# Reordering the products that run beside the second scan of a mixer layer

## The chip, the cores and the metric

The kernel runs on one core of one Trainium2 chip. The metric is the device time of one execution in microseconds (us). Three runs of the kernel before gave 2110.74, 2112.5 and 2116.45 us; the median is 2112.5 us.

## What is computed

The reference is a two-layer mixer block followed by an attention and mixture-of-experts block, for one sequence of 256 tokens and a width of 1024. The change touches only the two layers of the first block. There, one normalised input `u` is multiplied with the columns of one wide weight, and the pieces go to three branches whose results are gated and added:

```python
h = rmsnorm(x)                      # u in the kernel
z, xbc, dt, q, f, i, g, mq, mk, mv, ig, fg, mo, gates = split(h @ w_in)
y_ssd = ssd_branch(z, xbc, dt)      # two-way state space scan, then a gated norm
y_hg  = hgrn2_branch(q, f, i, g)    # two-way gated linear scan
y_ml  = mlstm_branch(mq, mk, mv, ig, fg, mo)
merged = (sigmoid(gate_s) * (y_ssd @ w_br_ssd)
          + sigmoid(gate_h) * (y_hg @ w_br_hg)
          + sigmoid(gate_m) * (y_ml @ w_br_ml))
x = x + merged @ w_out
```

The arithmetic is in fp32. The products written as `@` above are of 256 tokens with 1024 by 1024 slices of weights.

## The kernel before, in words

**Units.** All weights come from one stream in HBM, cut into units of 1 MB (128 partitions by 2048 numbers). A unit makes 256 output columns: it lands in one of four slots of `ring`, TensorE multiplies it with `u` or with a branch's result, the sum stands in one of three PSUM banks `G`, and ScalarE or VectorE reads it out and frees the bank. `KINDS` (line 49) is the list of units in order: `mq`, `mk`, `mv`, `mo` are the four inputs of the third branch, `gs` is the gate of the state space branch, `bs` its output weight, `gh` and `gm` are the other gates, `bh` and `bm` the other output weights. `OF`, `POS`, `USE` and the packing of the stream on the host follow from that list.

**Plain and split units.** A plain unit is 32 fp32 matmuls (line 1040, or 969 for the units that are laid out by token). A split unit is 48 faster matmuls in three groups of 16: high part of the weights by high part of `u`, high by low (both line 1030, or 1018 and 1023 for the first unit of a kind), and low part of the weights by high part of `u` (line 1035). For those, ScalarE copies the weights into a rounded high part (`hi`, line 2006, signal `whi_ok`) and VectorE subtracts it to get the low part (`lo`, line 2683, signal `wlo_ok`). TensorE waits for `whi_ok` ahead of the unit and for `wlo_ok` ahead of its last third. Line 2010 makes the high part of `u` (`u_high`) and line 2391 the low part (`u_low`). `mo`, `gs` and the first two `gh` are split (list `SCAN`, line 105); `mq`, `mk`, `mv` and `bs` are plain. `WSCAN` (line 326) says where in the arena each of these ten units has its high part.

**The second scan.** The hgrn2 branch is worked out in 18 levels k, nine for each half of the heads. Level k has arguments (`hgA`, VectorE lines 2541 to 2546), exponentials (ScalarE lines 1956 to 1958), operands (`hgB`, VectorE lines 2561 to 2564), small products (`hgB`, TensorE lines 1228, 1239, 1248) and a copy of the result (`hgC`, VectorE lines 2577 to 2600). After level 17 come the last output products (`ho`, TensorE line 1260, ScalarE line 1962), the squares (ScalarE line 1965), their sums (`hnorm`, TensorE line 1266), and on ScalarE four logarithms and four exponentials (lines 1969 and 1973), then on VectorE eight scalings and one multiplication (lines 2606 and 2610).

**The order by hand.** The order of all work of a layer is one list, `sched` (from line 632). Each engine walks through the same list and does its own part of every item. The part that matters is a loop over i from 2 to 23, one step for each of the units `mq + i`. In step i TensorE multiplies unit `mq + i`; VectorE does `hgA` of level i-1, `hgB` of level i-2 and `hgC` of level i-3; TensorE then does the small products of level i-2. At the end of a step the unit's bank is read (`read`). `hi` and `lo` of a unit stand one step ahead of it.

In the kernel before, steps 12 to 15 are the four `mo` units and steps 16 to 23 are `gs` and `bs` in turn:

```python
+ ["mq"] * 4 + ["mk"] * 4 + ["mv"] * 4 + ["mo"] * 4
+ ["gs", "bs"] * 4 + ["gh"] * 4 ...
```

So splits of weights stand in steps 11 to 15, 17, 19, 21 and 23. The sigmoid of all of `mo` (`msig`) stands in step 16. A `gs` unit is read by ScalarE, which writes its sigmoid to `MERGED`; a `bs` unit is then read by VectorE (line 2274), which multiplies it onto `MERGED`.

Of the kernel before, what the change touches and what calls it, by code (L numbers as in the profile page):

```python
# [20 lines left out]
ACT = mybir.ActivationFunctionType  # L21
AX_X = mybir.AxisListType.X

P = 128
D = 1024
# [24 lines left out]
         + ["mq"] * 4 + ["mk"] * 4 + ["mv"] * 4 + ["mo"] * 4  # L50
         + ["gs", "bs"] * 4 + ["gh"] * 4 + ["gm"] * 4 + ["bh"] * 4 + ["bm"] * 4
# [199 lines left out]
def program(nc, stream, par_d, con_d, x_d, par2_d, con2_d, out, upto=None):  # L251
    ctx = ExitStack()
    with ctx:
# [72 lines left out]
        WSCAN = (HF, 122, HF, 122, HF, HF, HF, HF, 42, 0)  # L326
# [106 lines left out]
        def signal(name, per_layer, credit=0):  # L433
            return Signal(sem(name), per_layer, credit)
# [50 lines left out]
        yln = signal("ssd_logs_ready", 1)  # L485
# [33 lines left out]
        merge_ok = signal("merged_ready", 4)  # L519
        silu_ok = signal("ffn_silu_ready", 22)  # L520
# [13 lines left out]
        lam_in, lam_mm, lam_exp = sem("lambda_products"), sem("lambda_sums"), sem("lambda_exponentials")  # L534
# [128 lines left out]
        gh, gs, mo = OF["gh"], OF["gs"], OF["mo"]  # L663
        for i in range(2, 24):
            if i in (17, 19, 21):
                sched.append(("hi", gs + i - 15))
            elif i == 23:
                sched.append(("hi", gh))
            elif 11 <= i <= 15:
                sched.append(("hi", mo + i - 11 if i < 15 else gs))  # L670
            if i == 12:
                sched.append(("u_low", 0))
# [35 lines left out]
            if k - 2 == 17:  # L708
                sched.append(("ho", 1))
# [1062 lines left out]
        def _(act):  # L1772
            st = Steps(act, act_step)

            def unit(lay, n):
                kind, j = KINDS[n], n - OF[KINDS[n]]
                j = j // 2 if kind in ("gs", "bs") else j
                if kind in ("rows", "bs", "bh", "bm", "out", "down") or kind in ("hi", "mv") and j % 2 == 0:
                    return
# [32 lines left out]
                else:  # L1812
                    dst = {"z": Z, "hf": HF, "hq": HQ, "hg": HG, "mq": MQ, "mk": MK, "mo": MO,
                           "gs": MERGED, "gh": GH, "gm": GM, "pleg": PLG}[kind]
                    func = {"z": ACT.Silu, "gs": ACT.Sigmoid, "gh": ACT.Sigmoid, "gm": ACT.Sigmoid,
# [32 lines left out]
            def item(kind, k, lay):  # L1848
# [114 lines left out]
                elif kind == "hnorm":  # L1963
                    act.wait_ge(ho_cp.sem, ho_cp.at(lay, 4))
                    act.activation(flat(HE[0], KC), flat(HQ, KC), ACT.Square).then_inc(hsq.sem, 1)
                    prime()
# [26 lines left out]
                elif kind in ("split", "hi"):  # L1993
# [101 lines left out]
            act.activation(small[:, 2:4], A[3][:, 0:2], ACT.Exp).then_inc(lam_exp, 1)  # L2095
# [127 lines left out]
        def _(dve):  # L2223
# [23 lines left out]
            def unit(lay, n):  # L2247
                kind, j = KINDS[n], n - OF[KINDS[n]]
                j = j // 2 if kind in ("gs", "bs") else j
                if kind not in ("rows", "bs", "bh", "bm", "out", "down", "xbc", "up"):  # L2250
                    return
# [10 lines left out]
                dve.wait_ge(unit_done.sem, unit_done.at(lay, POS[n] + 1))  # L2262
# [9 lines left out]
                elif kind == "bs":  # L2272
                    dve.wait_ge(*evac(lay, n - 1))
# [467 lines left out]
            dve.wait_ge(lam_exp, 1)  # L2741
# [503 lines left out]
```

## Time and profile before

| what | value |
| --- | --- |
| median of three runs | 2112.5 us |
| time of the profiled execution | 2116.87 us |
| span of its profile | 2114.8 us |
| TensorE busy with matmuls | 1969.2 us (93%) |
| VectorE busy | 1271.7 us (60%) |
| ScalarE busy | 930.9 us (44%) |
| mean busy share of the 16 DMA engines in the slices of the two layers | 3 to 6 tenths |

The profiled execution took 2.1 us more than its span, and is 4.4 us above the median of the three runs. Times in the timeline are counted from the start of the span. The second scan of the first layer lies at about 220 to 412 us, that of the second layer at about 977 to 1169 us.

In the timeline a row is: start, duration of the group, engine, line, operation, what it writes and reads, the number of instructions, and in brackets how long the engine had been idle before it and what released it. A group's duration runs to the modelled end of its last matmul, so it can overlap the start of the next row by 0.1 to 0.4 us; the distance between two starts is the safer measure. A row of stretches has, for each engine, busy us with the number of instructions, then the granted TensorE clock as a share of full speed, the share of the DMA engines and the GB/s.

### The profile page before, as it was taken

What the parts mean: (1) busy time and instruction counts of PE and PEld (TensorE: products, weight loads), DVE (VectorE), ACT (ScalarE), POOL (GpSimd) and SP (SyncE); (2) the same over time, 40 slices, a digit from 0 to 9 for tenths busy, and PEclk for the clock granted to TensorE, in tenths of its full rate; (3) what the DMA queues carried; (4) which work ended last, traced back from release to release, by engine and by line L of the source; (5) the groups of instructions that cost most, each with busy time, mean ns of one, the idle gap of its engine ahead of it and who ended that gap; (6) DMA issues with size and microseconds to landing.
All of it is one profiled execution on the core that took longest, in us unless ns stands there. A gap on an engine that the chain in (4) does not pass through costs nothing. (4 is left out here: it accounts for less than half of the span.)

```text
span 2114.8 us, 48552 instructions
## 1 busy us (share of the span) xinstructions
PE 1969.2 (93%) x20908; PEld 1702.5 (81%) x20908; DVE 1271.7 (60%) x2183; ACT 930.9 (44%) x1162; POOL 31.3 (1%) x62
## 2 busy tenths in 40 slices
PE   8999999999999999999999999999999897777766
PEld 7998869999999999988689999999987664444433
DVE  6887879488677567896795796786543211111111
ACT  5544655574556355546464754664412210111101
POOL 0000000000000000000000000000000000000000
PEclk9999999999999999999999999999999898888897
DMA  6555344444555554553434544455787899999997
GB/s 236 181 204 192 124 160 154 169 176 179 180 180 188 199 182 174 211 193 140 176 127 158 199 163 177 179 183 197 269 333 287 335 373 422 422 422 422 422 422 326
DMA packets 71935, 498.91 MB, mean 236 GB/s; under 512 B 8448, under 2 KB 8576, under 8 KB 13536
## 3 DMA queue, kind: packets, MB, share of 16 engines
q1 hardware_dynamic: 66528, 479.57, 59.5%
q0 software_dynamic: 4384, 14.49, 2.0%
q8 instruction: 128, 2.10, 0.4%
q10 hardware_dynamic: 864, 2.49, 0.3%
q14 instruction: 31, 0.25, 0.0%
HBM read 495.38 MB, written 1.15 MB: 235 GB/s over the span
## 5 line engine op out<-in xcount | busy, mean ns | idle before, releaser
L2683 DVE TENSOR_TENSOR ring_r<-ring,weights_and_u_split 128x2048 fp32r<-128x2048 f32 x88 | 201.4, 2291 | 76.4 <-ACT weights_and_u_split L2006 72.7
L1035 PE MATMUL bank<-weights_and_u_split,ring_r 128*128 128x256 f32 x1880 | 246.3, 283 | 0.0
L1035 PEld LDWEIGHTS bank<-weights_and_u_split,ring_r 128*128 128x128 f32 x1880 | 234.8, 192 | 0.0
L1030 PE MATMUL bank<-weights_and_u_split,hidden_and_weights_high 128*128 128x256 f32 x1664 | 211.5, 284 | 0.0
L1030 PEld LDWEIGHTS bank<-weights_and_u_split,hidden_and_weights_high 128*128 128x128 f32 x1664 | 203.6, 192 | 4.8 <-issue 4.3
L2006 ACT ACTIVATE weights_and_u_split<-ring 128x2048 fp32r<-128x2048 f32 x88 | 167.6, 1907 | 53.5 <-PE bank L1035 46.6
L3044 DVE COPY arena<-bank 128x128 f32<-128x128 f32 x32 | 9.3, 292 | 293.4 <-PE bank L1651 293.4
L2183 ACT ACTIVATE arena<-bank 64x256 f32<-64x256 f32 x32 | 12.1, 377 | 350.8 <-PE bank L1633 350.8
L1633 PE MATMUL bank<-arena 128*32 128x256 f32 x1312 | 109.1, 466 | 59.4 <-DMA arena<-stream 55.4
L2683 DVE TENSOR_TENSOR ring_r<-ring,hidden_and_weights_high 128x2048 fp32r<-128x2048 f32 x64 | 146.2, 2286 | 29.3 <-ACT hidden_and_weights_high L2006 29.2
L2239 DVE SCALAR_TENSOR_TENSOR arena<-bank,par,arena 128x255 f32<-128x255 f32 (+1 forms) x272 | 111.3, 476 | 48.7 <-ACT arena L1809 48.5
L1633 PEld LDWEIGHTS bank<-arena 128*32 128x32 f32 x1312 | 49.6, 126 | 111.6 <-issue 76.4
L2006 ACT ACTIVATE hidden_and_weights_high<-ring 128x2048 fp32r<-128x2048 f32 x64 | 121.9, 1907 | 11.9 <-PE bank L957 8.5
L1822 ACT ACTIVATE arena<-bank 128x512 f32<-128x512 f32 x96 | 56.9, 593 | 153.4 <-PE bank L1035 140.7
L1030 PE MATMUL bank<-weights_and_u_split 128*128 128x256 f32 x840 | 117.8, 283 | 0.0
L1809 ACT ACTIVATE arena<-bank,par 128x256 f32<-128x256 f32 x112 | 57.1, 559 | 130.4 <-PE bank L1035 127.6
L1040 PE MATMUL bank<-u,ring 128*128 128x256 f32 x512 | 114.0, 381 | 0.0
L1030 PEld LDWEIGHTS bank<-weights_and_u_split 128*128 128x128 f32 x840 | 108.3, 192 | 0.0
L1040 PEld LDWEIGHTS bank<-u,ring 128*128 128x128 f32 x512 | 96.3, 190 | 13.8 <-issue 0.8
L1030 PE MATMUL bank<-u_r,weights_and_u_split 128*128 128x256 f32 x736 | 103.3, 283 | 0.0
L1030 PEld LDWEIGHTS bank<-u_r,weights_and_u_split 128*128 128x128 f32 x736 | 94.9, 192 | 0.0
L1633 PE MATMUL bank<-ring,arena 128*32 128x256 f32 x672 | 53.7, 447 | 39.0 <-DMA ring<-stream 39.0
(492 smaller groups left out, 3636.5 us busy)
## 6 DMA issues: line engine op xcount, KB each, us to landing
ring<-stream SPq DMA_DIRECT2D x320, 1024.0 KB, 4.9
arena<-stream SPq DMA_DIRECT2D x129, 1024.0 KB, 25.9
arena<-rows_scratch POOLq DMA_DIRECT2D x48, 256.0 KB, 4.7
place_of_rows<-stream SPq DMA_DIRECT2D x2, 1024.0 KB, 6.1
place_of_parameters<-stream SPq DMA_DIRECT2D x2, 1024.0 KB, 8.0
h<-x_d ACTq DMA_DIRECT2D x4, 256.0 KB, 4.7
ring<-stream ACTq DMA_DIRECT2D x1, 1024.0 KB, 9.3
u<-stream SPq DMA_DIRECT2D x1, 1024.0 KB, 6.9
```

Of the source, the lines that this page charges most:

```text
L1030: pe.matmul(bank[:, c * S:(c + 1) * S], whi[k][:, c * P:(c + 1) * P], yhi[k] if xx is None else xx[:, k, :], start=(sub == 0 and c == part ...
L1035: mm = pe.matmul(bank[:, c * S:(c + 1) * S], wlo[k][:, c * P:(c + 1) * P], yhi[k] if xhi is None else xhi[:, k, :], start=False, stop=(end ...
L1040: mm = pe.matmul(bank[:, c * S:(c + 1) * S], w[:, k, c * P:(c + 1) * P], x[:, k, :], start=(k == 0), stop=(k == KC - 1))
L1633: mm = pe.matmul(G[0][g:g + 32, 0:S], xe[:, 2 * j + k, a * SLOTS:(a + 1) * SLOTS], w[k][:, g * 8:g * 8 + S], start=(j == k == 0), stop=(j ...
L1809: a = act.activation(arena[:, dst, :], bank[:, c * S:(c + 1) * S], ACT.Identity, scale=pc(wn, ch * width + width // 2), bias=pc(bn, ch))
L1822: act.activation(flat(at, 2), bank[:, :], func).then_inc(f.sem, 1)
L2006: act.activation(high(k), scan_high_or_low(k, ring[:, POS[k] % RING, :]), ACT.Copy).then_inc(whi_ok.sem, 1)
L2183: act.activation(arena[0:64, SGE, :], G[0][0:64, 0:S], ACT.Silu).then_inc(sg_ok, 1)
L2239: ins = stt(o, bank[:, c * S + lo + d:c * S + hi + d], pc(wn, chans[c] * width + j), o, ALU.mult, ALU.add)
L2683: tt(scan_high_or_low(k, ring_r[:, POS[k] % RING, :]), scan_high_or_low(k, w), high(k).bitcast(F32), ALU.subtract)\
L3044: V.tensor_copy(flat(HTE, 1)[:, 0:4 * SLOTS], A[4][:, 0:4 * SLOTS]).then_inc(ht_cp, 1)
```

## The change

The order of the units becomes `mq`, `mk`, `mv`, then four `bs`, four `mo`, four `gs`, `gh`. The splits of weights stand in steps 15 to 23, one in each. The high part of `u` is made in step 13 and not 10, its low part at the head of step 14 and not 12, and `msig` stands in step 20. `bs` is read by ScalarE with a plain copy to `MERGED`. ScalarE writes the sigmoid of a `gs` unit back into its PSUM bank, and VectorE multiplies the bank with `MERGED` and frees it. The squares of the hgrn2 output are an item of their own, `hsquare`, at the end of step 20, while `hnorm` stays at the end of step 21. The places of the high parts change with the order. A semaphore for the lambda exponentials of the second block is merged into another one.

```diff
-         + ["mq"] * 4 + ["mk"] * 4 + ["mv"] * 4 + ["mo"] * 4
-         + ["gs", "bs"] * 4 + ["gh"] * 4 + ["gm"] * 4 + ["bh"] * 4 + ["bm"] * 4
+         + ["mq"] * 4 + ["mk"] * 4 + ["mv"] * 4 + ["bs"] * 4 + ["mo"] * 4
+         + ["gs"] * 4 + ["gh"] * 4 + ["gm"] * 4 + ["bh"] * 4 + ["bm"] * 4
...
-        WSCAN = (HF, 122, HF, 122, HF, HF, HF, HF, 42, 0)
+        WSCAN = (HF, Z) * 4 + (42, 0)
...
         for i in range(2, 24):
-            if i in (17, 19, 21):
-                sched.append(("hi", gs + i - 15))
-            elif i == 23:
-                sched.append(("hi", gh))
-            elif 11 <= i <= 15:
-                sched.append(("hi", mo + i - 11 if i < 15 else gs))
-            if i == 12:
+            if i >= 15:
+                sched.append(("hi", mq + i + 1))
+            if i == 14:
                 sched.append(("u_low", 0))
...
-            if i == 16:
+            if i == 20:
                 sched.append(("msig", 0))
-            if i in (17, 19, 21):
-                sched.append(("lo", gs + i - 15))
-            elif i == 23:
-                sched.append(("lo", gh))
-            elif 11 <= i <= 15:
-                sched.append(("lo", mo + i - 11 if i < 15 else gs))
-            if i == 10:
+            if i >= 15:
+                sched.append(("lo", mq + i + 1))
+            if i == 13:
                 sched.append(("u_high", 0))
...
             if k - 2 == 17:
-                sched.append(("ho", 1))
+                sched += [("ho", 1), ("hsquare", 0)]
...
# ScalarE, unit
+                    if kind == "gs":
+                        act.activation(bank[:, :], bank[:, :], ACT.Sigmoid).then_inc(gs_sig.sem, 1)
+                        return
                     dst = {"z": Z, "hf": HF, "hq": HQ, "hg": HG, "mq": MQ, "mk": MK, "mo": MO,
-                           "gs": MERGED, "gh": GH, "gm": GM, "pleg": PLG}[kind]
+                           "bs": MERGED, "gh": GH, "gm": GM, "pleg": PLG}[kind]
...
# ScalarE, item
-                elif kind == "hnorm":
+                elif kind == "hsquare":
                     act.wait_ge(ho_cp.sem, ho_cp.at(lay, 4))
                     act.activation(flat(HE[0], KC), flat(HQ, KC), ACT.Square).then_inc(hsq.sem, 1)
+                elif kind == "hnorm":
                     prime()
...
-                    if k == OF["gh"]:
-                        act.wait_ge(unit_done.sem, unit_done.at(lay, POS[OF["gs"] + 6] + 1))
-                    elif k == OF["gh"] + 1:
-                        act.wait_ge(unit_done.sem, unit_done.at(lay, POS[OF["bs"] + 6] + 1))
+                    if k == OF["mo"] + 1:
+                        act.wait_ge(unit_done.sem, unit_done.at(lay, POS[last("bs")] + 1))
...
# VectorE, unit
+                if kind == "gs":
+                    dve.wait_ge(gs_sig.sem, gs_sig.at(lay, j + 1))
+                else:
+                    dve.wait_ge(unit_done.sem, unit_done.at(lay, POS[n] + 1))
...
-                elif kind == "bs":
-                    dve.wait_ge(*evac(lay, n - 1))
+                elif kind == "gs":
+                    dve.wait_ge(*evac(lay, OF["bs"] + j))
                     tt(flat(MERGED + 2 * j, 2), bank[:, :], flat(MERGED + 2 * j, 2), ALU.mult).then_inc(f.sem, 1)
```

## Rows read from the trace of the kernel before

**Rows 1.** Stretches of the second scan, first layer: busy us of each engine
```profile
340.00:350.00 10.00, 9.30 (x114) 8.39 (x114) 9.43 (x16) 8.86 (x9) 0.00 (x0) 1.00 0.29 107
...
370.00:380.00 10.00, 10.00 (x63) 9.27 (x63) 0.03 (x1) 3.65 (x5) 1.95 (x4) 1.00 0.43 152
```
**Rows 2.** Waits of TensorE, 285 to 450 us: total us, times, longest
```profile
PE banks_by_token L1228 <- DVE arena L2564: 1.3, 2, 0.7
```
**Rows 3.** Timeline of TensorE, first layer, steps 13 to 18
```profile
316.09 1.22 PE L1030 MATMUL bank<-weights_and_u_split,hidden_and_weights_high 128*128 128x256 f32 x8
...
322.04 0.76 PE L1228 MATMUL banks_by_token<-arena 128*32 128x32 f32 x64
...
336.03 0.76 PE L1228 MATMUL banks_by_token<-arena 128*32 128x32 f32 x64 [0.64 <-DVE arena L2564]
...
343.44 0.76 PE L1228 MATMUL banks_by_token<-arena 128*32 128x32 f32 x64 [0.69 <-DVE arena L2564]
344.13 7.17 PE L1040 MATMUL bank<-arena,ring 128*128 128x256 f32 x32
351.23 1.15 PE L1239 MATMUL banks_by_token<-arena 128*64 128x64 f32 x32
352.31 1.22 PE L1030 MATMUL bank<-weights_and_u_split,scan_weights_high 128*128 128x256 f32 x8
```
**Rows 4.** Timeline of TensorE, second layer: the wait of step 15
```profile
1092.90 0.76 PE L1228 MATMUL banks_by_token<-arena 128*32 128x32 f32 x64 [0.64 <-DVE arena L2564]
```
**Rows 5.** Timeline of VectorE, first layer, steps 12 to 17
```profile
305.42 2.50 DVE L2391 TENSOR_TENSOR u_r<-u,weights_and_u_split 128x512 fp32r<-128x512 f32 x4 [0.94 <-PE bank L969]
...
323.61 0.69 DVE L2541 TENSOR_TENSOR arena<-arena 128x512 f32<-128x512 f32 x1
...
331.02 0.69 DVE L2541 TENSOR_TENSOR arena<-arena 128x512 f32<-128x512 f32 x1
...
344.24 0.69 DVE L2541 TENSOR_TENSOR arena<-arena 128x512 f32<-128x512 f32 x1 [0.50 <-PE banks_by_token L1228]
...
348.51 0.68 DVE L2564 TENSOR_TENSOR arena<-arena 128x512 f32<-128x512 f32 x1
...
350.26 2.29 DVE L2683 TENSOR_TENSOR ring_r<-ring,scan_weights_high 128x2048 fp32r<-128x2048 f32 x1
352.46 0.68 DVE L2274 TENSOR_TENSOR arena<-bank,arena 128x512 f32<-128x512 f32 x1
```
**Rows 6.** Timeline of TensorE, first layer, two plain units of the early steps
```profile
255.48 7.17 PE L1040 MATMUL bank<-u,ring 128*128 128x256 f32 x32
...
263.28 7.17 PE L1040 MATMUL bank<-u,ring 128*128 128x256 f32 x32
```
**Rows 7.** Timeline of TensorE, first layer, steps 22, 23 and the unit behind
```profile
387.52 1.30 PE L1030 MATMUL bank<-weights_and_u_split,scan_weights_high 128*128 128x256 f32 x8
...
393.46 7.07 PE L1040 MATMUL bank<-arena,ring 128*128 128x256 f32 x32
400.18 1.30 PE L1030 MATMUL bank<-weights_and_u_split,scan_weights_high 128*128 128x256 f32 x8
```
**Rows 8.** Timeline of ScalarE, first layer, steps 21 to 23
```profile
387.91 2.42 ACT L1969 ACTIVATE arena<-banks_by_token,eps 128x512 f32<-128x512 f32 x4 [4.87 <-PE banks_by_token L1266]
390.36 2.19 ACT L1973 ACTIVATE arena<-arena 128x512 f32<-128x512 f32 x4
392.57 1.28 ACT L1822 ACT_TABLE_LOAD   x1
393.87 0.60 ACT L1822 ACTIVATE arena<-bank 128x512 f32<-128x512 f32 x1
394.36 1.91 ACT L2006 ACTIVATE scan_weights_high<-ring 128x2048 fp32r<-128x2048 f32 x1
```
**Rows 9.** Timeline of VectorE, first layer, the low part behind the normalisation
```profile
396.53 2.29 DVE L2683 TENSOR_TENSOR ring_r<-ring,scan_weights_high 128x2048 fp32r<-128x2048 f32 x1
```
**Rows 10.** Stretches with idle TensorE: in the third branch, and in the second block
```profile
490.00:496.00 6.00, 4.60 (x52) 3.71 (x56) 5.35 (x8) 2.31 (x3) 0.00 (x0) 1.00 0.36 109
...
1660.00:1670.00 10.00, 6.97 (x189) 5.05 (x180) 2.40 (x13) 4.32 (x12) 0.00 (x0) 0.81 0.36 130
```

More of the change, by code:

```diff
@@ L484, in program @@
         yrs = signal("ssd_rstd_ready", 1)
-        yln = signal("ssd_logs_ready", 1)
+        yln = signal("ssd_logs_then_lambda_exponentials_ready", 1)
         ys_fin = signal("ssd_branch_ready", 1)
@@ L519, in program @@
         merge_ok = signal("merged_ready", 4)
+        gs_sig = signal("state_gate_sigmoids_ready", 4)
         silu_ok = signal("ffn_silu_ready", 22)
@@ L533, in program @@
         ada_cp, ada_mm = sem("modulation_rows_copied"), sem("modulation_columns_ready")
-        lam_in, lam_mm, lam_exp = sem("lambda_products"), sem("lambda_sums"), sem("lambda_exponentials")
+        lam_in, lam_mm = sem("lambda_products"), sem("lambda_sums")
         rope_mm, rope_ok = sem("rope_turned"), sem("rope_done")
@@ L662, in program @@
                   ("hclamp", 0), ("ssd_add", 0), ("hlog", 0), ("ssd_log", 0), ("hsilu", 0), ("read", mq + 1), ("hgK", 0)]
-        gh, gs, mo = OF["gh"], OF["gs"], OF["mo"]
+        gh = OF["gh"]
         for i in range(2, 24):
-            if i in (17, 19, 21):
-                sched.append(("hi", gs + i - 15))
-            elif i == 23:
-                sched.append(("hi", gh))
-            elif 11 <= i <= 15:
-                sched.append(("hi", mo + i - 11 if i < 15 else gs))
-            if i == 12:
+            if i >= 15:
+                sched.append(("hi", mq + i + 1))
+            if i == 14:
                 sched.append(("u_low", 0))
@@ L1776, in unit @@
                 kind, j = KINDS[n], n - OF[KINDS[n]]
-                j = j // 2 if kind in ("gs", "bs") else j
-                if kind in ("rows", "bs", "bh", "bm", "out", "down") or kind in ("hi", "mv") and j % 2 == 0:
+                if kind in ("rows", "bh", "bm", "out", "down") or kind in ("hi", "mv") and j % 2 == 0:
                     return
@@ L2094, in _ @@
             act.wait_ge(lam_mm, 1)
-            act.activation(small[:, 2:4], A[3][:, 0:2], ACT.Exp).then_inc(lam_exp, 1)
+            act.activation(small[:, 2:4], A[3][:, 0:2], ACT.Exp).then_inc(yln.sem, 1)
             if upto == "ada":
@@ L2248, in unit @@
                 kind, j = KINDS[n], n - OF[KINDS[n]]
-                j = j // 2 if kind in ("gs", "bs") else j
-                if kind not in ("rows", "bs", "bh", "bm", "out", "down", "xbc", "up"):
+                if kind not in ("rows", "gs", "bh", "bm", "out", "down", "xbc", "up"):
                     return
@@ L2261, in unit @@
                     return
-                dve.wait_ge(unit_done.sem, unit_done.at(lay, POS[n] + 1))
+                if kind == "gs":
+                    dve.wait_ge(gs_sig.sem, gs_sig.at(lay, j + 1))
+                else:
+                    dve.wait_ge(unit_done.sem, unit_done.at(lay, POS[n] + 1))
                 bank, f = G[USE[n] % GBANKS], freed[USE[n] % GBANKS]
@@ L2740, in _ @@
             first_norm()
-            dve.wait_ge(lam_exp, 1)
+            dve.wait_ge(yln.sem, yln.at(DEPTH, 1))
             st.done(tt(small[:, 4:5], small[:, 3:4], small[:, 2:3], ALU.subtract))
@@ L3143, in layer_units @@
     parts = [packed] + [(units_by_token if k in ("hi", "mv") else units)(seg[k])
-                             for k in ("z", "xbc", "hf", "hq", "hi", "hg", "mq", "mk", "mv", "mo")]
-    parts.append(np.stack([units(g[:, :D]), units(i["w_br_ssd"][lay])], 1).reshape(8, P, UNIT))
-    parts += [units(w) for w in (g[:, D:2 * D], g[:, 2 * D:], i["w_br_hg"][lay], i["w_br_ml"][lay], i["w_out"][lay])]
+                             for k in ("z", "xbc", "hf", "hq", "hi", "hg", "mq", "mk", "mv")]
+    parts += [units(i["w_br_ssd"][lay]), units(seg["mo"])]
+    parts += [units(w) for w in (g[:, :D], g[:, D:2 * D], g[:, 2 * D:], i["w_br_hg"][lay], i["w_br_ml"][lay], i["w_out"][lay])]
     parts.append(units(i["w_up"][lay].reshape(D, 2, FC, P).transpose(0, 2, 1, 3).reshape(D, FC * UC)))
```

2 lines of the change are left out of this document (1 added, 1 removed).

## The prediction

> **What bounds the kernel now.** I read the chip's own busy shares first, then the stretches of the second scan, then the waits of TensorE in it, then the timeline of each engine step by step. The stretches say that TensorE is full: 10.00 of 10 us in most of them and 9.30 in the worst, at the full clock. VectorE is nearly full beside it in the middle of the scan (9.43 of 10) and empty near its end (0.03 of 10) [rows 1]. The waits say what is to be had: in the whole stretch that the change reorders TensorE waits 1.3 us, in two waits, both for the scan's operands from VectorE [rows 2]. They stand in steps 15 and 16, 0.64 and 0.69 us [rows 3], and the second layer has the same two; its first is again 0.64 us [rows 4]. So a layer has 1.33 us to give and two layers 2.7 us, 0.13% of the time. About 0.3%, 6.3 us, is what a measurement of this kernel can tell from no change. The change adds no matmul and takes none away, so whatever it wins has to be one of these waits, and whatever it loses a new one.
>
> Why TensorE waits there: a VectorE step with a weight split takes 7.41 us (331.02 less 323.61) [rows 5], a TensorE step with a split unit 5.95 us (322.04 less 316.09) and 0.69 us for the small products (344.13 less 343.44) [rows 3], together 6.64. VectorE falls behind by 0.77 us a step, and five such steps in a row are more than its head start.
>
> **The change, part by part.** I count for one layer, and take the profiled execution's own time, 2116.87 us, as the base of the sum; the difference then goes onto the median 2112.5.
>
> *Plain `bs` units in steps 12 to 15.* A plain step with small products is 7.80 us on TensorE (263.28 less 255.48) [rows 6], against a VectorE step without a split of 7.41 less some 2.2 us, 5.2 us. `u_low`, 2.50 us [rows 5], now falls into step 14, which makes that one 7.7: just covered by 7.80. `u_high` on ScalarE moves from step 10 to 13, where ScalarE has only the three exponentials and a read. VectorE therefore enters step 15 level with TensorE. The two old waits go: **-1.33 us**.
>
> *The splits in steps 15 to 18.* Put the start of unit 15 at 0. VectorE's step 15 takes 7.41; TensorE's plain step ends at 7.80. Step 16: VectorE 7.9 to 15.3, TensorE to 14.44. Step 17: operands are ready 4.95 us into VectorE's step (348.51 plus 0.68 less 344.24) [rows 5], at 20.25, and TensorE's unit ends at 20.39: still no wait. But this step has the long copy at the end of the small levels, so it takes 8.22 us (352.46 less 344.24) [rows 5] and ends at 23.5. TensorE's unit 18 starts at 20.39 + 1.08 (352.31 less 351.23) [rows 3] = 21.47 and ends at 27.42; the operands of level 16 are there at 23.5 + 4.95 = 28.45. **A new wait of 1.0 us** in step 18, behind VectorE's backlog: the queue is the same as before, only later. Behind it VectorE has no more arguments to make and catches up. Its bounds: 0 if VectorE's head start is a microsecond more than I think, 1.5 if step 14 does not quite hold `u_low`.
>
> *The last `gs` unit behind the normalisation.* Before, unit 23 is plain and needs nothing from the other engines. Now it is split, and its high part stands on ScalarE behind the four logarithms and four exponentials of `hnorm`. Put the start of unit 22 at 0 (387.52). The exponentials end at 390.36 + 2.19, that is 5.03 [rows 8]; the copy takes 1.91 [rows 8], to 6.93; TensorE is through with unit 22 at 5.94 (393.46 less 387.52) [rows 7]. **A new wait of 1.0 us**, with all later matmuls queued behind it. Then VectorE: it has the whole normalisation ahead of the low part, whose subtraction ends at 396.53 + 2.29, that is 11.30 [rows 9]. TensorE, started at 6.93, is through two thirds of the unit (3.97 of 5.95) at 10.90. **A second wait of 0.4 us.** Bounds for the two together: 0.9 (the copy overlaps the exponentials' end, and the subtraction is just in time) and 1.9 (a table load or a read slips in between).
>
> *What ScalarE and VectorE swap.* `bs` is read by ScalarE in steps with little work: 0.60 us each [rows 8], hidden by the plain unit. `gs` is held by a sigmoid of 0.60 and then a multiplication of 0.68 [rows 5, 8] and has two units' time, over 11 us, before its bank is needed; in step 22 VectorE comes to it at 11.3, behind the low part, and the bank is wanted by the second `gh` unit at about 19. Cost nothing; if that cover were gone it would be what VectorE is late. The sigmoid of the last `gs` unit stands ahead of the split of `gh` + 1, where a plain unit had no work on ScalarE: 0.60 us in front of a chain (split, decays, split, high part of `u`) whose end TensorE meets just in time after two more units. In the new kernel TensorE is itself later there. I take **+0.1 us**, bounds 0 and 0.6.
>
> *Squares ahead.* Left in `hnorm`, they would stand behind the read of unit 21, which now waits on ScalarE for TensorE to finish that unit; TensorE would then meet the sums without their input. Moved, they are done during unit 21. Nothing won against before, where TensorE did not wait there either.
>
> *Seams.* A plain unit ahead of scan products takes 7.11 us (7.80 less 0.69), one ahead of a split unit 6.72 (400.18 less 393.46) [rows 6, 7]; the four now all stand in the first place. The split units get part of it back. **+0.1 us**, bounds -0.3 and +0.7.
>
> *The table loads.* One is 1.28 us [rows 8]. They become fewer in steps 16 to 19 and stand where ScalarE has time. *The lambda semaphore, the places of the high parts, the order of the stream:* each unit's slot is still freed four units ahead, the same bytes move, and each place is still reused two units later; the first use of `Z` waits for the last `bs`, which is over as the split begins. Nothing. The gpsimd queue is not passed by anything: its rows for the third branch wait for the last output products, as before.
>
> Sum for a layer: -1.33 + 1.0 + 1.0 + 0.4 + 0.1 + 0.1 = +1.27 us; for two, +2.5 us. The profiled execution would go from 2116.87 to 2119.4, the median from 2112.5 to **2115.0 us**. The parts' bounds leave each layer between -0.7 (-1.33 + 0 + 0.9 + 0 - 0.3) and +3.4 (-1.33 + 1.5 + 1.9 + 0.6 + 0.7), so 2111.1 to 2119.3.
>
> **The rivals.** *Forecast, 0.63:* two old waits traded for later ones, a small loss, 2115.0.
>
> *Covered, 0.25.* The backlog does not build up, because VectorE enters step 15 early enough, and the normalisation's end leaves the last unit's high part in time. Then only the removal counts: -2.7 us, 2109.8. For it: the new order plainly spreads the splits, and steps 12 and 13 have over 2 us of slack each on VectorE. Against it: slack does not carry over, since `hgA` waits for the small products of two levels before, and ScalarE's queue is in order, so the copy cannot pass the exponentials [rows 8].
>
> *The clock falls, 0.07.* The place is step 23 (and 18), where TensorE now stands idle for 1.0 us in each. If the granted clock fell there, the units behind would run slower. The price from a row: a stretch of 10 us at a mean of 0.81 is 1.9 us of full-speed work lost [rows 10]; one at each of the four new places makes 7.6 us, and with the 2.5 us of waits +10.1 us, 2122.6. It decides as soon as such stretches cost over 1 us each. Against it: in the six us from 490, TensorE is idle for 1.40 and the clock stays at 1.00; it is 0.81 only where TensorE was busy for 7 of 10 us [rows 10]. The Trainium skill has the rule that speaks for this rival ("TensorE: Matmul & The Clock Gate", section "HAM oscillation — how this bites in real kernels"): idle gaps between groups of matmuls can throw the array back to half rate, and every following group starts cold. By that rule the time would be this rival's 2122.6; the trace does not show it at gaps of this size.
>
> *None of these, 0.05:* scatter of a median (the three runs differ by 5.7 us), half to either side.
>
> Faster by over 0.3% would be below 2106.2. No wait in the rows is large enough for it; I give 0.04 for scatter. Slower by over 0.3%, above 2118.8: the clock, and the top of my bounds, 0.09. The rest, 0.87, is the same. The range takes in the covered case and my own bounds and half a microsecond to a microsecond of scatter on either side: 2109.0 to 2120.0; the forecast's own range is 2111.1 to 2119.3.
>
> **What would show it.** Right: no wait of TensorE on line 2564 in the first two `mo` steps, one of about 1.0 us ahead of line 1239 in the step of the third `mo` unit; a wait of about 1.0 us on line 2006 ahead of the fourth `gs` unit and one of about 0.4 us on line 2683 inside it; from the first unit of the second scan to the first `gh` unit 1.3 us more than before, in both layers alike. Wrong: no wait there (then the time falls to 2110), a wait at the sums of squares on line 1266, a wait for a bank of `gs`, a granted clock under 1.00 between 300 and 420 us, or a wait of TensorE in step 14 for operands held up by `u_low`.

## The result, and the profile after

The changed kernel takes **2117.05 us** (median of 21 runs, 2110.99 to 2121.79), the kernel before 2112.0 us (21 runs beside them, 2107.94 to 2118.51). The ratio of the two is 1.0019, with a 95% interval of 1.001 to 1.0027: 4.0 us slower, between 2.1 and 5.7. By the bound of 0.3% that is no change that counts, and with this many runs it is still a small loss that is surely there. The forecast was 2115.0 and "a small loss". One execution of the kernel of experiment 8 took 4119.39 us; it stands in no median and no ratio here.

The waits of TensorE are the view that the forecast was about. This is the kernel after, from 220 to 480 us; the columns are engine and line, what it waited for, total us, times, longest us.

```profile
PE banks_by_token L1232 <- DVE arena L2560: 1.1, 1, 1.1
PE banks_by_token L1221 <- DVE arena L2560: 1.0, 2, 0.7
PE bank L1023 <- ACT hidden_low L2000: 0.8, 1, 0.8
PE bank L1028 <- DVE ring_r L2679: 0.4, 1, 0.4
PE bank L1011 <- ACT hidden_low L1901: 0.3, 1, 0.3
```

The numbers of lines are smaller than before by 7 on TensorE (1239 is now 1232, 1228 is 1221, 1030 is 1023, 1035 is 1028, 1018 is 1011), by 6 for the high part (2006 is 2000) and by 4 on VectorE (2564 is 2560, 2683 is 2679). The group of L1221 stands ahead of 285 us, in steps that the change leaves alone; the kernel before has it too (in the second layer it lists 2.3 us in 4 waits on that line, of which 1.33 are the two of the middle). So the two waits of [rows 2] are gone and four new ones stand there: 1.1, 0.8, 0.4 and 0.3 us. The second layer has the same list, with 0.9 for L1221. None of the waits is in step 14 (`u_low`), at the sums of squares or for a bank of `gs`, the three places that the forecast named as signs of being wrong.

The timeline of TensorE in the first layer, kernel after, shows where they are. The columns are start, duration, engine, line, operation, out<-in, and in brackets the idle time ahead of it and what ended it.

```profile
356.95 2.08 PE L1028 MATMUL bank<-weights_and_u_split,ring_r 128*128 128x256 f32 x16
360.13 1.15 PE L1232 MATMUL banks_by_token<-arena 128*64 128x64 f32 x32 [1.10 <-DVE arena L2560]
...
387.08 1.30 PE L1023 MATMUL bank<-weights_and_u_split,scan_weights_high 128*128 128x256 f32 x8
...
391.10 2.08 PE L1028 MATMUL bank<-weights_and_u_split,ring_r 128*128 128x256 f32 x16
393.97 1.22 PE L1023 MATMUL bank<-weights_and_u_split,hidden_low 128*128 128x256 f32 x8 [0.79 <-ACT hidden_low L2000]
...
398.43 2.18 PE L1028 MATMUL bank<-weights_and_u_split,ring_r 128*128 128x256 f32 x16 [0.36 <-DVE ring_r L2679]
400.45 1.12 PE L1023 MATMUL bank<-weights_and_u_split,scan_weights_high 128*128 128x256 f32 x8
...
413.26 2.91 PE L1011 MATMUL bank<-hidden_low,scan_weights_high 128*128 128x256 f32 x16 [0.26 <-ACT hidden_low L1901]
```

The first is in step 18, ahead of the small products. Then the last `gs` unit: TensorE waits for its high part, starts it at 393.97, does two thirds, and waits again, until 398.43, for its low part. The fourth is ahead of the split of `u` for the third branch.

ScalarE and VectorE at the last `gs` unit, kernel after, same columns:

```profile
387.47 2.42 ACT L1965 ACTIVATE arena<-banks_by_token,eps 128x512 f32<-128x512 f32 x4 [1.57 <-PE banks_by_token L1259]
389.92 2.19 ACT L1969 ACTIVATE arena<-arena 128x512 f32<-128x512 f32 x4
392.02 1.90 ACT L2000 ACTIVATE hidden_low<-ring 128x2048 fp32r<-128x2048 f32 x1
...
396.09 2.28 DVE L2679 TENSOR_TENSOR ring_r<-ring,hidden_low 128x2048 fp32r<-128x2048 f32 x1
```

Logarithms, exponentials and the copy of the high part stand one behind the other without a gap (387.47 to 393.92), and TensorE starts 0.05 us behind the copy. The subtraction ends at 398.37, and TensorE goes on at 398.43. Both queues run in order, and the normalisation stands ahead in each.

The stretches of the kernel after at the two places; the columns are stretch, its length, busy us (instructions) of TensorE, weight loads, VectorE, ScalarE and GpSimd, the granted clock, DMA share and GB/s.

```profile
356.00:362.00 6.00, 4.90 (x64) 4.63 (x63) 5.96 (x9) 4.23 (x5) 0.00 (x0) 1.00 0.38 111
392.00:398.00 6.00, 5.21 (x42) 4.87 (x41) 5.96 (x7) 5.61 (x5) 0.00 (x0) 1.00 0.50 175
```

The clock stays at 1.00 in both, which is 2.4 GHz, and so does its mean over the whole of 20 to 1640 us.

**Where the time went.** Differences of starts in the timeline of TensorE, between marks that both kernels have, tell more than idle rows. The marks of the first layer are the first `ho` product (306.00 before, 304.72 after) and the first product of the third branch (411.88 and 411.97, line 1278 or 1271). I take the same pair in the second layer, and from the first mark on to the router's products, where the next part begins.

| us | layer 1 | layer 2 | first `ho` to router | router to end | span |
|---|---|---|---|---|---|
| before | 105.88 | 105.87 | 1338.04 | 470.76 | 2114.8 |
| after | 107.25 | 107.24 | 1341.52 | 464.96 | 2111.2 |

The change costs 1.37 us in each layer and 3.48 us up to the router. The part behind the router, which the change does not touch, was 5.8 us shorter in the profiled execution of after, so that its span is the shorter one although the kernel is slower. That part was between 463.0 and 470.8 us in the twelve traces of this study, whatever the kernel. Two traces of one kernel (experiments 2 and 3) differ by 0.17 us from the first `ho` product to the router and by 2.6 us behind it. So from here on I compare traces up to the router and whole kernels by their ratios. A single time says little: 21 runs of the kernel before are spread over 10.6 us.

### The profile page after: what moved, and what is told of

Its sections match the earlier page's. It is cut to its first block and busy times, and to the rows that moved or that the text cites. A ratio compares the mean times of both kernels' runs of the same rounds, so it can differ in the third digit from the quotient of the medians.

```text
span 2111.2 us, 48556 instructions
## 1 busy us (share of the span) xinstructions
PE 1963.3 (93%) x20908; PEld 1697.2 (80%) x20908; DVE 1271.7 (60%) x2183; ACT 930.9 (44%) x1166; POOL 31.4 (1%) x62
## 3 DMA queue, kind: packets, MB, share of 16 engines
HBM read 495.38 MB, written 1.15 MB: 235 GB/s over the span
## 5 line engine op out<-in xcount | busy, mean ns | idle before, releaser
L1023 PE MATMUL bank<-weights_and_u_split,hidden_and_weights_high 128*128 128x256 f32 x1600 | 202.1, 284 | 0.0
L1023 PEld LDWEIGHTS bank<-weights_and_u_split,hidden_and_weights_high 128*128 128x128 f32 x1600 | 195.4, 192 | 4.7 <-issue 4.3
L2679 DVE TENSOR_TENSOR ring_r<-ring,hidden_and_weights_high 128x2048 fp32r<-128x2048 f32 x60 | 137.0, 2286 | 29.1 <-ACT hidden_and_weights_high L2000 29.0
L2000 ACT ACTIVATE hidden_and_weights_high<-ring 128x2048 fp32r<-128x2048 f32 x60 | 114.4, 1908 | 12.9 <-PE bank L950 8.5
```

The costliest lines, as they stand in the source:

```text
L1023: pe.matmul(bank[:, c * S:(c + 1) * S], whi[k][:, c * P:(c + 1) * P], yhi[k] if xx is None else xx[:, k, :], start=(sub == 0 and c == part ...
L2000: act.activation(high(k), scan_high_or_low(k, ring[:, POS[k] % RING, :]), ACT.Copy).then_inc(whi_ok.sem, 1)
L2679: tt(scan_high_or_low(k, ring_r[:, POS[k] % RING, :]), scan_high_or_low(k, w), high(k).bitcast(F32), ALU.subtract)\
```

## Experiments

**The theory:** the order of work on ScalarE and VectorE makes the loss. The two parts (high and low) of unit 23's weights stand behind the normalisation (about 1.15 us of waiting a layer), VectorE's backlog stands in step 18 (1.1 us), and the old waits (1.33 us) went since there are plain units there. **The rivals:** the order of units itself (the seams between split and plain ones) costs time; a wait sets the clock down; or these waits cover each other, so that taking one away only moves it.

**1. Squares back in the normalisation.** What did the squares' new place buy?

```
             if k - 2 == 17:
-                sched += [("ho", 1), ("hsquare", 0)]
+                sched.append(("ho", 1))
             if k - 3 == 17:
-                sched.append(("hnorm", 0))
+                sched += [("hsquare", 0), ("hnorm", 0)]
```

> The new order with the squares put back to the head of hnorm, behind the read of unit 21. My theory: ScalarE's queue is in order, so the squares start only when TensorE is through with unit 21 and its sigmoid is read (0.58 us), and take 1.91 us; TensorE then waits about 2.5 us ahead of the sums of squares in each layer, the rest of the chain moves back with it, and the waits ahead of and inside the last gs unit stay at 0.8 and 0.4 us. From the head of the output products of the first half to the first gh unit a layer takes 2.5 us more than in the changed kernel. Rival (the squares were never at stake, as TensorE did not wait for them before the change either): no wait there, no difference.

Measured: 2125.13 us beside 2113.32 of the kernel before, one run each. ScalarE's and TensorE's rows at the sums, and the stretches around them, in this kernel; the last stretch is the one behind the same wait in layer 2:

```profile
384.62 1.90 ACT L1960 ACTIVATE arena<-arena 128x2048 f32<-128x2048 f32 x1
386.58 5.19 PE L1259 MATMUL banks_by_token<-arena,con 128*128 128x256 f32 x16 [2.48 <-ACT arena L1960]
```

```profile
384.00:387.00 3.00, 0.52 (x2) 0.42 (x2) 0.69 (x1) 2.85 (x3) 0.00 (x0) 0.86 0.57 171
387.00:390.00 3.00, 3.00 (x9) 2.38 (x9) 0.00 (x0) 0.83 (x1) 0.00 (x0) 0.57 0.44 186
390.00:393.00 3.00, 3.00 (x21) 2.79 (x20) 0.00 (x0) 1.20 (x3) 0.00 (x0) 1.00 0.00 0
...
1151.00:1154.00 3.00, 3.00 (x9) 2.37 (x8) 0.00 (x0) 0.00 (x0) 0.00 (x0) 0.50 0.10 41
```

The wait of 2.48 us is as forecast. But a layer is 4.2 us longer than in the kernel after (111.46 against 107.25), not 2.5. The rest is the granted clock: 0.57 (near the lower level of 1.2 GHz) in the three us from 387, where the wait has just ended (386.58), so that the 16 sums take 5.19 us, against 3.62 in the kernel after. That is 1.6 us more for the same matmuls. So the rival of the falling clock was a real one, only not at the waits that this change makes. And the squares' place is a needed part of the new order: without it the two layers lose 8.7 us more (1350.21 less 1341.52).

**2 and 3. The last split ahead of the normalisation.** The high and the low part of unit 23 are moved from behind `hnorm` to just ahead of it. Nothing else changes. The third run is the same kernel with more executions.

```
-            if i >= 15:
+            if i >= 15 and i != 22:
                 sched.append(("hi", mq + i + 1))
...
-            if i >= 15:
+            if i >= 15 and i != 22:
                 sched.append(("lo", mq + i + 1))
...
             if k - 3 == 17:
-                sched.append(("hnorm", 0))
+                sched += [("hi", mq + i + 2), ("lo", mq + i + 2), ("hnorm", 0)]
```

> The new order with the split of the last gs unit, high and low part, put ahead of the normalisation on ScalarE and VectorE. My theory: the waits of 0.79 and 0.36 us ahead of and inside that unit go, in both layers, since the copy (1.9 us) now runs while TensorE forms the sums of squares (3.3 us); the logarithms may start 0.3 us later, which nobody meets. A layer is 1.1 to 1.2 us shorter. Rival (the normalisation is the limit): the wait moves to the first gh unit or to the third branch, and the layer is no more than 0.3 us shorter.

> The changed kernel with only the last gs unit's split put ahead of the normalisation, timed. Its trace, with one wait of 1.07 us and one of 0.26 us left, had the stretch from the first output product of the second scan to the third branch of the second layer at 862.5 us, against 862.7 before and 865.9 in the changed kernel. Expected: within 0.1% of the kernel before, that is, the loss of the change is gone with this one placement. Rival (the loss is in the order or in the tail, not in these waits): 0.1% to 0.2% slower than before, as the changed kernel.

Measured: 2109.67 us beside 2113.32 in the first, one run each; in the second 2112.85 us (12 runs, 2108.99 to 2117.76) beside 2112.61 of before (29 runs): ratio 1.0001, 0.9991 to 1.0012. The waits of TensorE from 300 to 420 us in it:

```profile
PE banks_by_token L1232 <- DVE arena L2560: 1.1, 1, 1.1
PE bank L1011 <- ACT hidden_low L1901: 0.3, 1, 0.3
```

Both waits of unit 23 are gone, and nothing took their place. A layer falls from 107.25 to 105.55 us, by 1.70 where 1.1 to 1.2 was expected, and the stretch to the router from 1341.52 to 1338.14, which is that of before (1338.04). So moving one split gives back as much as the change lost: 3.4 us in the trace, 3.8 by the ratios (0.0018 of 2112, each of the two ratios uncertain by about 0.001). The waits of step 18 and behind the scan are still there; the two old waits that went pay for them.

**4. The low part of the third `mo` unit on GpSimd.** Does VectorE's backlog make the wait of step 18? If so, 2.3 us less for VectorE should end it. In the kernel after, VectorE leaves out the subtraction of that unit, and GpSimd's queue, which is free there, does it with the same two semaphores (VectorE also waits for it ahead of its next subtraction, which the cut below leaves out):

```
+                k = OF["mo"] + 2
+                pool.wait_ge(wlo_ok.sem, wlo_ok.at(lay, NTH_SPLIT[k]))
+                pool.wait_ge(whi_ok.sem, whi_ok.at(lay, NTH_SPLIT[k] + 1))
+                pool.tensor_tensor(scan_high_or_low(k, ring_r[...]), scan_high_or_low(k, ring[...]),
+                                   high(k).bitcast(F32), ALU.subtract).then_inc(wlo_ok.sem, 1)
```

> The new order with the low part of the third mo unit's weights (128x2048, one subtraction) made by the idle gpsimd engine and not by VectorE. My theory, a backlog of VectorE: without 2.2 us of its step, the wait of 1.1 us ahead of the small products of level 16 goes; a layer is 1.1 us shorter, as long as the gpsimd subtraction takes under 9 us. Rival 1 (the wait is for something else, the exponentials or the copy of two levels before): it stays. Rival 2 (the gpsimd engine is slow or disturbs VectorE in SBUF): VectorE's own instructions beside it get longer than 0.69 and 1.22 us, or TensorE waits for the low part inside that unit, by the gpsimd duration less 9 us.

Measured: 2128.08 us beside 2113.32, the opposite of what the theory forecast, with a wait of 4.16 us. Rows of GpSimd, VectorE and TensorE in it:

```profile
348.04 4.66 POOL L892 TENSOR_TENSOR ring_r<-ring,scan_weights_high 128x2048 fp32r<-128x2048 f32 x1 [176.59 <-ACT scan_weights_high L2005]
348.28 4.97 DVE L2546 TENSOR_TENSOR arena<-arena 128x512 f32<-128x512 f32 x1
353.18 0.68 DVE L2547 TENSOR_TENSOR arena<-arena 128x512 f32<-128x512 f32 x1
355.51 0.68 DVE L2565 TENSOR_TENSOR arena<-arena 128x512 f32<-128x512 f32 x1
356.25 1.98 PE L1237 MATMUL banks_by_token<-arena 128*64 128x64 f32 x32 [4.16 <-DVE arena L2565]
```

The same operands and the same products in the kernel after:

```profile
351.16 0.68 DVE L2560 TENSOR_TENSOR arena<-arena 128x512 f32<-128x512 f32 x1
351.93 1.15 PE L1232 MATMUL banks_by_token<-arena 128*64 128x64 f32 x32
```

A subtraction of 128x512 that takes VectorE 0.69 us takes 4.97 us while GpSimd subtracts: it ends 0.55 us behind GpSimd's end (348.28 and 4.97 is 353.25, GpSimd's is 352.70). This is the second rival of the expectation. VectorE was not made lighter: 2.3 us were taken off it and 4.3 us added, and the added part comes first. The wait is one step ahead of the one in question, in step 17. There TensorE had its operands just in time (351.84, and the products start at 351.93); now they come at 356.19. The last row of this kernel shows a second thing, 1.98 us for 32 small products that take 1.15 in the kernel after. The stretches of this kernel:

```profile
352.00:356.00 4.00, 0.09 (x1) 0.00 (x0) 4.00 (x5) 2.11 (x4) 0.70 (x1) 0.87 0.63 219
356.00:360.00 4.00, 3.75 (x40) 3.64 (x41) 3.01 (x7) 2.27 (x2) 0.00 (x0) 0.50 0.12 47
360.00:364.00 4.00, 4.00 (x29) 4.00 (x28) 4.00 (x7) 2.10 (x3) 0.00 (x0) 0.77 0.00 0
```

The clock is down again, behind a wait of 4.16 us. In step 18 TensorE then waits no more, but that does not answer the question: its unit starts 5.1 us later than in the kernel after (358.15, not 353.01) and VectorE's step only 3.2 (358.27, not 355.11). The run shows that a VectorE later by 4.35 us makes TensorE wait 4.16 us in step 17. What a lighter VectorE does to the wait of step 18 was not seen here.

**5. The same in the kernel before**, with the fourth `mo` unit, which stands ahead of the two old waits.

> The kernel before with the low part of the fourth mo unit's weights made by the gpsimd engine. Backlog theory: both old waits, 0.64 and 0.69 us in steps 15 and 16, go, in both layers, 1.33 us a layer, if the gpsimd subtraction takes under 8.5 us. Rival (gpsimd slow or disturbing): a wait of TensorE for the low part inside the fourth mo unit takes their place.

Measured: 2119.11 us beside 2113.32. The row of VectorE in it, and its wait:

```profile
324.17 4.97 DVE L2550 TENSOR_TENSOR arena<-arena 128x512 f32<-128x512 f32 x1
```

```profile
PE banks_by_token L1233 <- DVE arena L2569: 4.2, 1, 4.2
```

4.97 us again, to the hundredth. TensorE does not wait inside the `mo` unit, as the rival had it, but ahead of the small products of step 14. The two waits of [rows 3] are not in its list from 285 to 450 us: they stand behind this one, which put TensorE back more than VectorE, and there VectorE waits for TensorE (0.84 and 1.32 us). GpSimd is no helper for VectorE in either order.

**6. Operands of the second scan first (after).** Another way to bring the operands earlier: in each step `hgB` of the level that TensorE needs next goes ahead of `hgA` of the one behind it. No work is added.

```
             k = i - HG_DELAY
+            if 0 <= k - 1 < HSTEPS:
+                sched.append(("hgB", k - 1))
             if 0 <= k < HSTEPS:
...
-            if 0 <= k - 1 < HSTEPS:
-                sched.append(("hgB", k - 1))
             if i == 9:
```

> The new order, with VectorE making the operands of level k-1 ahead of the arguments of level k in every step of the second scan (two items of the list swapped, the same work). Backlog theory: the wait of 1.1 us ahead of the small products of level 16 is VectorE's lateness of about 1 us at the end of a queue that has 2.5 us of arguments in front of the operands; with the operands 2.5 us earlier in the step it goes, and so do the two waits of 0.68 and 0.27 us of the early steps: 2.0 us less in a layer, of which 1.1 between the output products and the third branch. Rival (the operands wait for the exponentials, which now end late): the waits stay or new ones appear in steps without a split, by up to 1.8 us each.

Measured: 2123.37 us (one run) beside 2111.69 (18 runs). All waits for scan operands are gone, the one of step 18 as well, and a layer falls from 107.25 to 106.08 us. That answers what the fourth run left open: with the same work in another order on VectorE the wait goes. Only the 0.8 and the 0.4 of unit 23 are left in the scan. But a new one of 4.2 us a layer stands in the early steps. The next run shows it.

**7. The same swap in the kernel before**, timed.

> The kernel before with the same swap of two items. Backlog theory: its four waits in a layer (0.68, 0.27, 0.64 and 0.69 us) go, 2.3 us a layer, 4.6 us in all, 0.22% faster; the stretch from the output products to the third branch is 1.3 us shorter in each layer. Rival: exponentials late, no gain.

Measured: 2119.82 us (12 runs, 2116.39 to 2127.47) beside 2111.69 (18 runs), ratio 1.004, 1.0026 to 1.0053: 0.4% slower where 0.22% faster was expected. The rows of ScalarE and TensorE around its only wait:

```profile
269.50 0.63 ACT L1956 ACTIVATE arena<-arena 128x512 f32<-128x512 f32 x1 [5.02 <-DVE arena L2546]
...
271.62 1.28 ACT L1947 ACT_TABLE_LOAD   x1
...
276.53 0.58 ACT L1822 ACTIVATE arena<-bank 128x512 f32<-128x512 f32 x1
277.16 6.36 PE L969 MATMUL bank<-ring,u 128*128 128x512 f32 x8 [4.19 <-ACT arena L1822]
```

and the stretches there:

```profile
275.00:278.00 3.00, 0.84 (x1) 0.50 (x2) 2.67 (x6) 2.98 (x3) 0.00 (x0) 0.62 0.00 0
278.00:281.00 3.00, 3.00 (x5) 1.28 (x4) 0.46 (x1) 2.50 (x4) 0.00 (x0) 0.50 0.00 0
281.00:284.00 3.00, 3.00 (x22) 1.21 (x23) 1.97 (x3) 0.00 (x0) 0.00 (x0) 0.74 0.00 0
```

In step 7 ScalarE has the step's three exponentials, then two long logarithms (`hlog` of the scan's second half, lines 1947 and 1948) with a table load, then the read of the unit's bank. That order is the same in both kernels. But with the swap VectorE makes the arguments behind the operands, so the exponentials start 8.03 us behind the start of the unit (269.50 less 261.47), where they start 3.13 us behind it in the kernel before (266.41 less 263.28), and the read comes later with them. TensorE wants that bank, waits 4.19 us, and the clock falls to 0.50: eight matmuls take 6.36 us, where they take 3.60 in the kernel before (274.61 to 278.21). The stretch of the scan itself is what the swap was made for: from the first `ho` product to the third branch it takes **104.40 us in both layers**, 1.48 less than before. The two waits that it took away have 1.33 us in their rows.

**8. Swap and early split together (after), timed.**

> The new order with the swap and with the last gs unit's split ahead of the normalisation. If the waits are all that can be mended, a layer is 1.1 + 0.95 + 0.79 + 0.36 us = 3.2 us shorter than in the changed kernel. Against the kernel before with the swap (all waits of both scans gone) it is then still behind by what the order itself costs TensorE, the seams and the 0.26 us behind the scan: 0.5 us a layer by the two traces, 0.1 us by my prediction. Rival (the new order frees something further on): it is level or ahead.

Measured: 2121.34 us (median of six runs, 2117.55 to 2123.81) beside 2111.69, ratio 1.0044, 1.0028 to 1.0059; the same wait of 4.2 us for the bank. Its layer takes 104.42 us, against 104.40 of the seventh run. With no wait left between these two marks the two orders of units are equal, to 0.02 us a layer. That is the answer on the seams: no cost can be seen. What the new order still has is the wait of 0.3 us behind the third branch's first product, outside these marks; up to the router it is 0.3 us longer in all (1341.59 against 1341.28).

**9 and 10. The swap without steps 7 to 10** (the logarithms stand in step 7), in the kernel before and in the kernel after with its early split. Both differ from runs 7 and 8 in one condition each:

```
-            if 0 <= k - 1 < HSTEPS:
+            if 0 <= k - 1 < HSTEPS and not 7 <= i <= 10:
                 sched.append(("hgB", k - 1))
...
-            if 0 <= k - 1 < HSTEPS:
+            if 0 <= k - 1 < HSTEPS and 7 <= i <= 10:
                 sched.append(("hgB", k - 1))
```

> The kernel before with operands ahead of arguments, but not in steps 7 to 10. The swap in step 7 put the exponentials, and behind them two logarithms, two table loads and the read of that step's bank later on ScalarE, and TensorE waited 4.2 us for the bank. Without it there I expect no wait of TensorE in either second scan: 2.3 us less in a layer than in the kernel before, 4.6 us in all, 0.2% faster. Rival: the waits of the steps that are swapped come back as bank waits elsewhere; then the time is the kernel's before or longer.

> The new order with operands ahead of arguments (not in steps 7 to 10) and the last gs unit's split ahead of the normalisation. Expected: no wait in the second scan, 3.2 us less in a layer than in the changed kernel, 6.4 us in all, so 2.9 us (0.14%) faster than the kernel before; but 0.4 to 0.6 us a layer behind the kernel before with its own swap, which is the price of the order itself. Rival: level with it.

Measured: the kernel before with the swap 2112.28 us (12 runs, 2108.39 to 2115.19), ratio 0.9996, 0.9986 to 1.0007: no difference that these runs can tell, where 4.6 us less was expected. The kernel after with swap and early split **2109.53 us** (12 runs, 2106.44 to 2113.94) beside 2112.61: ratio **0.9981, 0.9971 to 0.9992**. That is 4.0 us less, between 1.7 and 6.1, where 2.9 was expected. It is the fastest here and the only one whose interval lies below 1. The traces up to the router explain only 1.1 us of it (1338.04 less 1336.93); where the rest comes from, if it is more than scatter, is open. The waits of TensorE in it, from 220 to 480 us:

```profile
PE banks_by_token L1223 <- DVE arena L2562: 0.9, 1, 0.9
PE bank L964 <- ACT arena L1819: 0.9, 1, 0.9
PE bank L1013 <- ACT hidden_low L1903: 0.3, 1, 0.3
```

No wait was expected in either kernel. The first two are where the order of the two items changes back, at step 7; both kernels have them, and without them both might gain some 1.8 us a layer more. No run shows that. The table of the traces, in us ("both" is the swap and the early split together):

| kernel | layer 1 | layer 2 | first `ho` to router |
|---|---|---|---|
| squares back | 111.46 | 111.67 | 1350.21 |
| last split ahead | 105.55 | 105.58 | 1338.14 |
| last split ahead, second trace | 105.57 | 105.57 | 1338.31 |
| low part on GpSimd | 112.74 | 112.94 | 1352.86 |
| before, low part on GpSimd | 109.75 | 109.95 | 1346.30 |
| operands first | 106.08 | 106.07 | 1345.58 |
| before, operands first | 104.40 | 104.40 | 1341.28 |
| both | 104.42 | 104.42 | 1341.59 |
| before, operands first, not in steps 7 to 10 | 104.39 | 104.39 | 1336.07 |
| both, not in steps 7 to 10 | 104.42 | 104.41 | 1336.93 |

By this table the kernel before with the swap is 0.86 us shorter up to the router than the one that measured fastest, 0.43 us a layer, which is the price of the order that was expected (0.4 to 0.6). Nearly all of it lies behind the third branch's first product, where the wait of 0.26 us stands. By the medians the kernel before with the swap is 2.75 us slower. The intervals of the ratios overlap, so which of the two is faster stays open.

## Why the prediction was right, and where its terms were off

The forecast was the right case, and each of its waits stands where it was put, on the line and in the step that were named. The range of 2109.0 to 2120.0 took in the covered case too, so the time alone could not have told the two apart; the waits do. The whole was 1.5 us short by the ratio: +2.5 us forecast, +4.0 measured (2.1 to 5.7), 3.5 in the traces.

- *The old waits go, -1.33 us.* Right in place. By starts it is 1.48 a layer (105.88 less 104.40).
- *From the first unit of the second scan (unit 2) to the first `gh` unit, +1.3 us.* 1.56 in both layers (before 223.31 to 400.18, after 222.02 to 400.45). The next units, which now follow a split one, give 0.18 back up to the third branch.
- *Step 18, +1.0 us.* 1.10 in the row, and 1.18 by starts (353.01 to 360.13 is 7.12, the step before it 5.94). The working by VectorE's steps holds as well: its steps start at 339.47, 346.89 and 355.11 in the kernel after, 7.42 and 8.22 us apart, where the forecast took 7.41 and 8.22.
- *Unit 23, +1.0 and +0.4 us.* 0.79 and 0.36 in the rows, 0.95 and 0.72 by starts (387.08, 393.97 and 400.45, against 5.94 and 5.76 for such a unit without a wait). Both ends of the chain (copy behind the exponentials, subtraction behind the normalisation) are as forecast: 6.84 and 11.29 us behind the start of unit 22, where it had 6.93 and 11.30, and run 2 shows that their place is the cause.
- *Three waits together.* 2.4 us forecast, 2.25 in the rows, but **2.83 by starts** (107.25 less the 104.42 of the same units without them). This is where the sum was short, above all in the second wait of unit 23 (0.4 forecast, 0.72 measured) and in step 18. The old waits were priced at their idle rows, and a wait costs more than that: in the rows a group of matmuls reaches past the start of the next (398.43 and 2.18 is 400.61, but the next starts at 400.45), and the idle time ahead of a wait is counted from that late end. The group behind a wait is also 0.1 us longer between starts (398.43 to 400.45 is 2.02, where 404.29 to 406.21 is 1.92). Unit 23's two waits show both together: 1.15 us in the rows, 1.70 us won by removing them. Less the old waits' 1.48, the difference is 1.35 us a layer instead of 1.07.
- *Behind the scan, +0.1 us (0 to 0.6).* The place was the right one: a wait of 0.26 us for the split of `u`. By starts it is 0.37 us a layer: half of what 3.48 leaves above twice 1.37. The place itself shows 0.42 in the first layer (411.97 to 413.26 after, 411.88 to 412.75 before). The value that I took was the mis-sized term here, its bounds held it. That the sigmoid of the last `gs` unit delays that split was argued, and no run takes it away alone.
- *Seams, +0.1 us.* Not seen: 0.02 us (runs 7 and 8), inside the bounds of the term.
- *Squares ahead, 0.* Right for the kernel as it is. The forecast gave no price for the case without it; it is 4.2 us a layer, wait and clock together (run 1).
- *Table loads, semaphore, places, DMAs, gpsimd queue, 0.* Nothing in the rows speaks against it: no wait for a transfer or a slot in the scans.

Sum by starts: -1.48 + 2.83 + 0.02 + 0.37 = +1.74 a layer, +3.5 for two, against +1.27 and +2.5 forecast. (It has to meet the traces' 3.48, as its last term is the remainder.)

**The rivals.** *Covered* (2109.8) fell: the backlog did build up and the copy could not pass the exponentials, the two reasons given against it. *The clock falls* (2122.6) did not happen: 1.00 in both stretches with the new waits. It did in the experiments: in stretches behind waits of 2.48, 4.16 and 4.19 us the clock was 0.57, 0.50 and 0.50, and the matmuls there took up to 1.8 times as long. The rule of the Trainium skill that spoke for this rival ("TensorE: Matmul & The Clock Gate", section "HAM oscillation — how this bites in real kernels") is borne out by those traces, and not at the shorter waits of the kernel after. The rival's price of 1.9 us a fall was near: 1.6 us more for the sums behind the wait of 2.48 us, 2.8 us more for the eight matmuls behind the one of 4.19 us. Up to the router a fall goes with the length of the wait in all these traces: one at each wait of 2.48 us and more, none at the shorter ones. The longest of those stand outside the scans, in every kernel: in the kernel after 1.46 us at 773.7 and 1.77 us at 1630.0, with the clock at 1.00. No wait lay between 1.77 and 2.48 us. The row against the rival (1.40 us idle in six at a clock of 1.00, [rows 10]) was above the size that the change makes.

## What to carry to other kernels

When work is reordered among engines whose queues run in order, ask for each split, copy or read what long chain now stands ahead of it: moving one split from behind a chain of logarithms and exponentials to ahead of it gave back the whole loss here, while the order of the units itself won nothing once the waits were gone (0.02 us a layer in the scan, and still a wait of 0.26 us behind it). Within a step, the item whose result TensorE needs next goes first, unless a bank read stands behind it; such a swap has to be looked at in every step that has other work. Price a wait by the starts on both sides of it, not by its idle row, and ask of a longer one on TensorE whether it costs clock as well: here waits of 2.48 us and more did, and waits of up to 1.77 us did not.

## What the runs showed of the hardware that was not expected

- **A two-input instruction of GpSimd held one of VectorE until it had ended**: 4.97 us instead of 0.69, in two kernels and both layers of each, beside 4.66 us on GpSimd for what VectorE does in 2.28.
- **TensorE's clock fell with a wait of 2.48 us** in a scan where it was at 1.00 till then: 0.86 in the three us of the wait, 0.57 in the next three, 1.00 again from 390 us. A wait of 1.10 us, and one of 0.79 with 0.36 four us later, left it at 1.00, and so did one of 1.77 us ahead of the router.
- **The part behind the router** took 463.0 to 470.8 us in twelve traces of kernels that are the same there, more scatter than the whole effect of this change.
